# Three products of rounded parts for the sparse-attention scores of heads 1 to 11, tiles 1 to 3

## What is computed

```python
qh = q.reshape(B_, S, NSA_KV, NSA_HPG, NSA_DH).transpose(0, 2, 3, 1, 4).astype(jnp.float32) * (NSA_DH ** -0.5)
...
ss = jnp.einsum('bghqd,bgqkd->bghqk', qb, kg) + bias_s
ps = masked_softmax(ss, (rel_s >= 0)[:, :, None])
osel = jnp.einsum('bghqk,bgqkd->bghqd', ps, vg)
...
sw = jnp.einsum('bghqd,bgkd->bghqk', qb, kwb) + head_bias(rel_w)
pw = masked_softmax(sw, mask_w)
ow = jnp.einsum('bghqk,bgkd->bghqd', pw, vwb)
return gb[:, 0, ..., None] * oc + gb[:, 1, ..., None] * osel + gb[:, 2, ..., None] * ow
```

## Time and profile before

| | |
|---|---|
| median of 3 runs | 2342.91 us (2341.49 to 2344.74) |
| the profiled execution | 2339.77 us, span 2337.7 us |
| PE busy over the span | 2226.8 us (95%) |
| DVE busy | 820.4 us (35%) |
| ACT busy | 504.4 us (22%) |
| loop at issue | about 783 to 929 us of the span |
| in 790 to 931 us: PE, DVE, ACT busy | 130.78, 118.40, 69.63 of 141 us |

### The profile page before, as it was taken

One profiled execution on the slowest core, in us unless ns is written; L12 is line 12 of the kernel. 1 busy time (PEld: TensorE's weight loads), 2 busy tenths in 40 slices (PEclk: granted clock), 3 DMA queues, 4 the chain that ended last, 5 costly groups with the idle time before them and its releaser, 6 DMA issues. The chain is left out here.

```text
span 2337.7 us, 32450 instructions
## 1 busy us (share of the span) xinstructions
PE 2226.8 (95%) x13844; PEld 1652.4 (71%) x13844; DVE 820.4 (35%) x1668; ACT 504.4 (22%) x885; POOL 210.0 (9%) x173
## 2 busy tenths in 40 slices
PE   8999999999999998999989999999999999998987
PEld 5888888888888777878877876555565555555553
DVE  6453245243225688453256561111111111111113
ACT  3221333231223554242224220000000000000001
POOL 0640000011100000750000000000000000000000
PEclk9999999999999999999999999999999999999999
DMA  8633222354331100435163689999999999999997
GB/s 260 231 122 126 72 85 91 100 167 151 116 96 28 42 24 27 175 124 167 59 129 127 250 344 409 427 426 427 427 426 427 427 427 426 427 426 427 428 426 313
DMA packets 123829, 573.29 MB, mean 245 GB/s; under 512 B 30488, under 2 KB 44428, under 8 KB 97784
## 3 DMA queue, kind: packets, MB, share of 16 engines
q1 hardware_dynamic: 110468, 533.21, 58.2%
q0 software_dynamic: 12064, 33.79, 4.1%
q10 hardware_dynamic: 1152, 4.19, 0.5%
HBM read 543.63 MB, written 39.47 MB: 249 GB/s over the span
## 5 line engine op out<-in xcount | busy, mean ns | idle before, releaser
L525 PE MATMUL ps<-w_parts,u_parts 128*128 128x512 f32 (+2 forms) x1920 | 414.6, 376 | 2.9 <-DVE u_parts L713 2.6
L525 PEld LDWEIGHTS ps<-w_parts,u_parts 128*128 128x128 f32 x1920 | 349.2, 188 | 61.2 <-DVE u_parts L713 3.1
L3254 PE MATMUL ps<-mem,mem_u 128*64 128x256 f32 x2464 | 291.4, 390 | 4.5 <-issue 2.8
L490 DVE TENSOR_TENSOR w_parts<-w_raw,w_parts 128x2048 fp32r<-128x2048 f32 (+2 forms) x70 | 161.8, 2311 | 321.1 <-ACT w_parts L485 321.1
L3377 DVE TENSOR_TENSOR mem_c<-mem_c,ps 128x256 f32<-128x256 f32 x64 | 26.9, 421 | 684.9 <-PE ps L3254 678.7
L3254 PEld LDWEIGHTS ps<-mem,mem_u 128*64 128x64 f32 x2464 | 181.2, 135 | 110.2 <-issue 17.1
L485 ACT CAST w_parts<-w_raw 128x2048 fp32r<-128x2048 f32 (+2 forms) x70 | 128.6, 1837 | 399.4 <-PE ps L525 166.3
L3281 PE MATMUL ps<-mem,mem_c 128*64 128x512 f32 x624 | 194.7, 625 | 20.1 <-DMA mem<-in_expert_w_down 11.2
L1569 PE MATMUL ps<-w_parts,u_parts 128*128 128x512 f32 x768 | 181.6, 393 | 0.4 <-DVE u_parts L1598 0.4
L1569 PEld LDWEIGHTS ps<-w_parts,u_parts 128*128 128x128 f32 x768 | 142.2, 188 | 29.8 <-issue 0.8
L523 PE MATMUL ps<-u_parts,w_parts 128*128 128x512 f32 x672 | 154.5, 390 | 1.7 <-DVE w_parts L490 1.7
(11 more groups left out here) (447 smaller groups left out, 2675.3 us busy)
## 6 DMA issues: line engine op xcount, KB each, us to landing
mem<-in_expert_w_gate SPq DMA_DIRECT2D x39, 2048.0 KB, 35.6
mem<-in_expert_w_up SPq DMA_DIRECT2D x38, 2048.0 KB, 40.7
mem<-in_expert_w_down SPq DMA_DIRECT2D x37, 2048.0 KB, 40.9
mem_u<-in_expert_w_up SPq DMA_DIRECT2D x26, 2048.0 KB, 40.5
mem_u<-in_expert_w_down SPq DMA_DIRECT2D x19, 2048.0 KB, 42.1
mem_c<-in_expert_w_gate SPq DMA_DIRECT2D x13, 2048.0 KB, 36.0
mem_u<-in_expert_w_gate SPq DMA_DIRECT2D x12, 2048.0 KB, 36.6
w_raw<-in_od_w_in SPq DMA_DIRECT2D x21, 1024.0 KB, 5.1
```

What stands on the lines that cost most here:

```text
L490: dve.tensor_tensor(self.part(n, 1), self.raw(n), self.part(n, 0).bitcast(F32), ALU.subtract).then_inc(self.low, 1)
L525: mm = pe.matmul(out, u[:, x, ku, g.t * P:(g.t + 1) * P], w[y][:, kk, :], start=first, stop=last)
L3254: mm = pe.matmul(ps[SLOTS * h:SLOTS * (h + 1), bank, 0:256].rearrange("s (c j) -> s c j", j=2), x[:, kk, :], w[:, kk, :].rearrange("p (c h ...
```

## The change

Heads 1 to 11 in tiles 1 to 3 get their scores from three fp32r products (high q x high k, high q x low k, low q x high k) that accumulate in PSUM. Head 0, and tile 0 of every head, keep the fp32 product. Four things come with it:

- the keys are split once: four ACT casts of 128 x 512 after the exponentials of step 0, and four DVE subtractions after the lows of step 1;
- the queries of head h + 1 are split while head h runs: an ACT cast of 128 x 512 at the end of the iteration with t = 1, a DVE subtraction of 128 x 512 after the lows with t = 2 (buffers for two heads);
- the copies of the turned weights of tiles 0 and 1 are no longer shared: ACT takes both branches in one instruction, after both have been turned, and DVE copies nothing for these tiles. Tiles 2 and 3 stay shared;
- the waits of PE for the copies follow this.

```diff
+    PRODUCTS = ((0, 0), (0, 1), (1, 0))
...
+    def by_dve(v):
+        whole, rest = divmod(v + 1, NT)
+        return 2 * whole + max(0, rest - 2)
...
                     for i, kT in enumerate((k.ksT, k.kwT)):
-                        pe.matmul(k.ps[:, 2 * (u % 2) + i, 0:m], k.qT[:, h, t * P:(t + 1) * P], kT[:, g, 0:m],
-                                  start=True, stop=True).then_inc(scored, 1)
+                        o = k.ps[:, 2 * (u % 2) + i, 0:m]
+                        if h == 0 or t == 0:
+                            mm = pe.matmul(o, k.qT[:, h, t * P:(t + 1) * P], kT[:, g, 0:m], start=True, stop=True)
+                        else:
+                            pe.wait_ge(k_low, 2 * NKV)
+                            pe.wait_ge(q_low, h)
+                            for x, z in PRODUCTS:
+                                mm = pe.matmul(o, q_parts[x][:, h % 2, t * P:(t + 1) * P],
+                                               k_parts[z][:, NKV * i + g, 0:m], start=x + z == 0, stop=x == 1)
+                        mm.then_inc(scored, 1)
...
                     pe.wait_ge(cop_a, v + 1)
-                    pe.wait_ge(cop_v, v + 1)
+                    if by_dve(v):
+                        pe.wait_ge(cop_v, by_dve(v))
...
             def take_turned(v):
                 w = (steps[v][1] + 1) * P
-                act.wait_ge(turned, 2 * v + 1)
+                both = steps[v][1] < 2
+                act.wait_ge(turned, 2 * v + 1 + both)
                 if v >= 2:
                     act.wait_ge(mixed, v - 1)
-                act.copy(pT[v % 2][:, 0:w], k.ps[:, 4, 0:w]).then_inc(cop_a, 1)
+                if both:
+                    act.copy(pT[v % 2].rearrange("p (i w) -> p i w", i=2)[:, :, 0:w], k.ps[:, 4:6, 0:w]).then_inc(cop_a, 1)
+                else:
+                    act.copy(pT[v % 2][:, 0:w], k.ps[:, 4, 0:w]).then_inc(cop_a, 1)
+
+            def split_keys():
+                act.wait_ge(ma.mixed, len(ma.steps))
+                for i, kT in enumerate((k.ksT, k.kwT)):
+                    for g in range(NKV):
+                        act.copy(k_parts[0][:, NKV * i + g, :], kT[:, g, :]).then_inc(k_high, 1)
+
+            def split_head(h):
+                if h >= 3:
+                    act.wait_ge(scored, 2 * NT * (h - 1))
+                act.copy(q_parts[0][:, h % 2, :], k.qT[:, h, :]).then_inc(q_high, 1)
...
+                    h, t = steps[u]
+                    if u == 0:
+                        split_keys()
+                    if t == 1 and h + 1 < NH:
+                        split_head(h + 1)
...
-                if 2 <= u < n + 2:
+                    if u == 1:
+                        for i, kT in enumerate((k.ksT, k.kwT)):
+                            for g in range(NKV):
+                                dve.wait_ge(k_high, NKV * i + g + 1)
+                                dve.tensor_tensor(k_parts[1][:, NKV * i + g, :], kT[:, g, :],
+                                                  k_parts[0][:, NKV * i + g, :].bitcast(F32), ALU.subtract).then_inc(k_low, 1)
+                    if t == 2 and h + 1 < NH:
+                        dve.wait_ge(q_high, h + 1)
+                        dve.tensor_tensor(q_parts[1][:, (h + 1) % 2, :], k.qT[:, h + 1, :],
+                                          q_parts[0][:, (h + 1) % 2, :].bitcast(F32), ALU.subtract).then_inc(q_low, 1)
+                if 2 <= u < n + 2 and steps[u - 2][1] >= 2:
                     v = u - 2
                     w = (steps[v][1] + 1) * P
-                    if v >= 2:
-                        dve.wait_ge(mixed, v - 1)
+                    dve.wait_ge(mixed, v - 1)
                     dve.wait_ge(turned, 2 * v + 2)
                     dve.tensor_copy(pT[v % 2][:, 512:512 + w], k.ps[:, 5, 0:w]).then_inc(cop_v, 1)
```

More of the change, by code:

```diff
@@ L1920, in nsa @@
     bias_loaded = [k.sem(f"nsa_bias{i}") for i in range(2)]
+    q_high, q_low, k_high, k_low = (k.sem("nsa_" + x) for x in ("q_high", "q_low", "keys_high", "keys_low"))
+    q_parts = [rounded(k, f"nsa_q_{x}", N0 + 1024 * i, 2, S) for i, x in enumerate(("high", "low"))]
+    k_parts = [rounded(k, f"nsa_keys_{x}", o, 2 * NKV, S) for x, o in (("high", Z0 + 11264), ("low", Z0 + 8192))]
+    PRODUCTS = ((0, 0), (0, 1), (1, 0))
     c_uses = [("score", t) for t in range(NT)]
@@ L2046, in _ @@
                         pe.wait_ge(exped, 2 * v + 1 + i)
-                        if v:
-                            pe.wait_ge(cop_v if i else cop_a, v)
+                        if i and v and steps[v - 1][1] >= 2:
+                            pe.wait_ge(cop_v, by_dve(v - 1))
+                        elif v:
+                            pe.wait_ge(cop_a, v)
                         for kt in range(t + 1):
```

## The result

The changed kernel takes 2347.61 us in the median of 21 runs (2343.92 to 2352.27), the kernel before 2341.95 us in 21 runs beside it. The ratio is 1.0032, with a 95% interval from 1.0025 to 1.0039: a small loss, 7.5 us by the ratio and 5.7 by the medians. The profiled execution took 2345.0 us, with a span of 2343.0 (before: 2337.7).

The account below looks back on a forecast made before the run. The prediction took a closed ring of dependences through PE, DVE and ACT, 11.86 us per head, to bound the loop. 2.3 + 2.5 + 0.04 gave +4.8 us on 2342.91, so 2347.7 us, range 2342 to 2351.5.

Parts of the forecast that it names:

- The ring: From mix 1 to the next head's, dependences through PE, DVE and ACT set 11.86 us, faster scores gain nothing; chance 0.60.
- The terms of the ring: Per head, DVE's subtraction for copy 0 and its wait +0.03, ACT's wider copy 1 +0.22: 12.11 us for ten turns.
- The start: Ahead of the loop's first mix 1, the keys' split and first queries' subtraction delay it by 2.3 us.
- The last head, nothing net: In the last head no next one is split: copy 0's 0.21 saved, the wider copy 1 costs 0.22.
- The sum: Whole kernel: start 2.3, ten turns 2.5 and first turn 0.04 make +4.8 us.
- After the loop nothing I can see takes it back.: Behind the loop, `odd_out` starts where the loop ends, so the loop's added time stays.
- PE's work counts: Rival for the loop: time follows PE's work, -6.7 us for scores, +2.3 for the start, 2338.5 us; chance 0.12.
- The additions hide: Rival: the wider copy costs nothing in the loop's heads, only the start's delay is left, 2345.2 us; chance 0.14.
- they cost more: Rival: ACT's two-bank copy or colliding subtraction adds 0.15 to 0.35 us per head, 2349.5 to 2351.5; chance 0.13.
- the clock falls: Rival: PE waits more in the loop and drops to 1.2 GHz, +9 us per head, near 2440; chance 0.01.

Follow-up runs that it names:

- e1: The changed kernel with every score again one fp32 product, splits and wider ACT copies kept; ratio 1.0019 to the kernel before.
- e8: The kernel before with only the keys' split added (four ACT casts, four DVE subtractions), its result unused; ratio 1.0004 to the kernel before.
- e3: The kernel before with ACT copying both branches of tile 0 alone, no split and no rounded products; ratio 0.9981 to the kernel before.
- e11: e7 with fp32 scores everywhere, all splits kept; ratio 0.9991 to the kernel before.
- e7: The changed kernel with the queries' subtraction at t = 3 and ACT's copy ahead of its first exponential; ratio 0.9993 to the kernel before.
- e2: The kernel before with ACT copying both branches of tiles 0 and 1, no split and no rounded products; ratio 0.9991 to the kernel before.
- e9: The changed kernel with 59 redundant PE wait instructions in the later fourier and ssm stage; ratio 1.0064 to the kernel before.
- e5: The changed kernel with 59 redundant PE wait instructions in the loop, ahead of mix 1; ratio 1.0031 to the kernel before.
- e6: The changed kernel with the queries' subtraction moved from the lows of t = 2 to those of t = 3; ratio 1.0010 to the kernel before.
- e10: e7 with 59 redundant PE wait instructions in the later fourier and ssm stage; ratio 1.0016 to the kernel before.

## Why the prediction was right, point by point

- *The ring, scores in it nowhere.* Right. Products or none, 12.10 us (after, e1). The saving on PE was 0.24 + 0.14 + 0.14 = 0.52 us a head by the starts of scores 3, 2 and 1 (805.23 to about 806.02 against 0.93), expected 0.61, and it went into the wait ahead of mix 1: 1.21 us, expected near 1.3.
- *The terms of the ring*, +0.03 for the subtraction in place of wait and copy 0, +0.22 for the wider copy: 12.11 expected, 12.10 measured. ACT's copy over two banks costs what a plain one of 512 elements does, 0.56 us.
- *The start*, +2.3: measured +2.24. e8 has +1.9 for the keys alone; the rest comes with the first queries' split and the wider copy 1, which no run takes apart.
- *The last head, nothing net*: -0.34 us. Too small to matter, but not nothing.
- *The sum*, +4.8: the loop has +4.43.
- *"After the loop nothing I can see takes it back."* Nothing was given back, but something was added: about 3 us, which I hadn't looked for, since the change touches nothing there. The change adds 66 matrix instructions (three for each product of rounded parts where an fp32 product has two), 66 loads of weights and 65 waits to PE's stream, 197 in all, and I costed them by their time alone. They move the place of one block of instructions: its packet takes 1.80 us in place of 0.99, and PE waits 3.62 us for it in place of 1.16. That the median came out at 2347.61 against 2347.7 is partly luck: the loss is 5.7 us by the medians and 7.5 by the ratio where 4.8 was worked out, and the median of the kernel before stood a microsecond lower in the 21 runs than in the three I started from.
- *PE's work counts.* Wrong for this change (e1), but true 0.3 us further down: in e3 and e11 PE is in the ring. The section "TensorE Precision Notes" of the page "FP8 and Floating Point Precision" of the Trainium skill counts four passes for true fp32, of which the change keeps three. The direction is borne out for PE's work, the size isn't: scores 3 take 1.48 us for 1.72, a seventh less and not a quarter. For the time it counts only in e7 against e11.
- *The additions hide, they cost more, the clock falls.* None did. The granted clock was 1.00 through the loop, with PE busy for 126.39 of 145 us.

## What to carry to other kernels

When a wait comes back in every round with the same length, add up the ring that it closes before you make any engine's work cheaper, and then look for the second ring: here it lay only 0.3 us below the first, so that e2 brought 0.26 us a head of 0.36 expected, and e3 0.34 of 0.58. Work that has to be added to an engine in the ring costs by its place: the same subtraction cost 0.6 us a head more at t = 2 than at t = 3. And count what an edit adds to an engine's stream of instructions, since the price can come in a later stage where transfers fill the DMA engines.

## What the runs showed of the hardware that was not expected

- PE waited up to 6.3 us for one block of 256 of its own instructions, in a stage with full DMA engines, and went on 1.40 to 1.76 us after the end of the block's packet in each of the fourteen traces.
- A wait instruction of PE for what has long happened isn't free: 59 in a row stood 0.106 us apart (e9). In e5 three of them, behind the wait that counts, delayed what follows by 0.3 us.
- ACT copies 128 x 2 x 256 elements out of two PSUM banks in 0.56 to 0.59 us and 128 x 2 x 384 in 0.80, one instruction each.
- The first eight products of 33x512 of an execution (L900, at 14 us) took 3.65 to 4.13 us in ten of the fourteen traces, and 7.00 in four of them (e5, e6, e10, e11), whichever the kernel. Everything behind them is 3 to 4 us later in those, which is why loops are compared from their own first product. The granted clock reads 1.00 in 14 to 16 us of both kinds; the cause isn't known.
